# Thirty-two more bytes ahead of the weight tiles: where matmul operands start in SBUF

## The chip, the cores and the metric

The kernel runs on one core of one Trainium2 chip. The metric is the device time of one execution in microseconds (us). Three runs of the kernel before are shown, and their median is taken.

## What is computed

Two transformer blocks run one after the other on 256 tokens of width 1024, all in float32. Cut to its large products:

```
# block 1
u    = rms_norm(x, g_norm_mix);  proj = u @ w_in + b_in              # 1024 x 5408
y_m  = mlstm_mixer(...proj...);  y_n = nsa_mixer(...proj...)
x    = x + sum(sigmoid(merge) * (ys @ w_branch)) @ w_out
f    = rms_norm(x, g_norm_ffn)
x    = rms_norm(x + (silu(f @ w_gate) * (f @ w_up)) @ w_down, g_final)
# block 2
h    = rms_norm(x, g_mix_2);     z = h @ w_in_2                      # 1024 x 9304
o_gla, o_dsa, o_mem = gated linear attention, sparse attention, attention over mem
x    = x + sum(sigmoid(gate_i) * (o_i @ w_o_i)) @ w_out_2
x    = x + moe(rms_norm(x, g_ffn_2))                                 # 16 experts, 2 of one group of 4
```

## The kernel before

**Slabs.** Every large weight matrix is read in slabs of 1024 x 256 values (1 MB; 8 KB a partition). A slab lands in `ring` (four slots, `RAW`). ScalarE makes its high part `w_hi` by a copy to the rounded format fp32r (three slots, `HI`; line 580, `high`), and VectorE the low part `w_lo = ring - w_hi` over `ring` itself (line 588, `low`). The operand on the other side is kept as two such parts as well (`xT_hi`, `xT_lo`, and in other stages `ysT`, `mixT`, `memT`, `h`, `o_m`, `o_g`, `o_d`, `merged`, `xgs`, `xgo`, `turned`). TensorE adds three products for every pair, high by high, high by low, low by high (`product`, line 612, so that nearly all matmuls have this one line):

```
for m, (a, b) in enumerate(((ah, bh), (ah, bl), (al, bh))):
    ins = pe.matmul(dst, a, b, ...)      # a is loaded as 128 x 128 weights, b moves through
```

**Three ways round.** `slab_rows` loads a piece of the slab as weights and moves 256 columns of `xT` (or `ysT`, `o_m`, `o_g`, `o_d`) through it. `slab_tokens` loads a piece of the activations and moves 256 columns of the slab. `slab_wide` (stages `vo`, `memk`, `memkv`, `mq`, `gvg`, `dq`), the down projections of the FFN and the experts load activations and move 512 columns of the slab. In a profile's row the moving operand stands first: `bank<-xT_hi,w_hi` moves `xT_hi` over weights from `w_hi`.

**Stages.** `STREAM` fixes the order of the slabs: `qk`, `nq`, `kv`, `vo`, `merge`, `branch`, `out`, `memk`, then the FFN (33 slabs), `memkv` to `dq`, gates and output products of block 2, `out2`, and the experts (60 slabs). Each engine has its own program in this order. SyncE issues the loads (lines 1050 and 1117), each when a counter of slabs that TensorE is done with (`slab_used`) says that a slot is free. In the expert stage more slots are added (`ring_more`, `w_lo_more`, `w_hi_more`).

**Where tiles lie.** `sb(name, shape)` takes the next free bytes of each partition, rounded up to 32. All tiles up to `ss` have sizes that are multiples of 64 bytes. `ss` holds eight sums of squares (with the means and roots made of them) and takes 32 bytes. Behind it come `ring` (over which `w_lo` lies), `w_hi`, and the region that both blocks share, in which `place(offset, ...)` puts tiles at given distances from its start. So in the program as built (byte in the partition, and the remainder by 64 and by 256):

| tile | before | by 64 | by 256 | with the change | by 64 | by 256 |
|---|---|---|---|---|---|---|
| `x` | 22,784 | 0 | 0 | 22,784 | 0 | 0 |
| `xT_hi` | 39,168 | 0 | 0 | 39,168 | 0 | 0 |
| `xT_lo` | 47,360 | 0 | 0 | 47,360 | 0 | 0 |
| `ss` | 55,552 | 0 | 0 | 55,552 | 0 | 0 |
| `ring`, `w_lo` | 55,584 | 32 | 32 | 55,616 | 0 | 64 |
| `w_hi` | 88,352 | 32 | 32 | 88,384 | 0 | 64 |
| the region's start | 112,928 | 32 | 32 | 112,960 | 0 | 64 |
| `ysT_hi` | 209,312 | 32 | 160 | 209,344 | 0 | 192 |
| `mixT_lo` | 166,272 | 0 | 128 | 166,304 | 32 | 160 |

`memT`, `h`, `turned`, `xgs`, `xgo`, `o_m`, `o_g`, `o_d`, `merged`, `mixT_hi` and `ysT_lo` have the same remainders as the region's start. Pieces of a slab (1024 bytes apart, 512 within one) and of the activations (512 or 1024 apart) keep the remainder of their tile. `mixT_lo`, `qk`, `sig`, `v1` and `c1`, and a score of tiles of up to 128 bytes, lie behind tiles whose size is an odd multiple of 32 and so have the other remainder than the region.

Of the kernel before, what the change touches and what calls it, by code (L numbers as in the profile page):

```python
# [14 lines left out]
P = 128  # L15
T = 256
TT = T // P
# [113 lines left out]
def program(nc, dram, out, plan):  # L131
# [3 lines left out]
    def sb(name, shape, dtype=F32, into=None):  # L135
        return (into or ctx).enter_context(nc.sbuf_tensor(name, shape, dtype))
# [32 lines left out]
    with ExitStack() as into:  # L169
        xT_raw = sb("xT_raw", [P, KT, T], into=into)  # L170
    xT_lo = sb("xT_lo", [P, KT, T], F32R)
    ss = sb("ss", [P, 4 * TT])
    raw_ctx = ExitStack()
    ring = sb("ring", [P, RAW, KT, SW], into=raw_ctx)
    raw_ctx.close()
# [2928 lines left out]
```

How the kernel before makes its waits and increments, by code:

```python
    def evicted(eng, s):  # L540
        for w in all_out(s):
            eng.wait_ge(*w)
# [1 line left out]
    def slab_out(eng, name, j=0):  # L544
        eng.wait_ge(slab_used, SLAB[name] + j + 1)
# [23 lines left out]
    def high(act, end):  # L570
        for s in range(split["hi"], end):
            act.wait_ge(*loaded(s))
            if HI <= s < MOE + HI:
                act.wait_ge(slab_used, s - HI + 1)
            elif MOE + HI <= s < MOE + MORE_HI:
                act.wait_ge(*moe_pe.done("gather", KT - 1))
            elif s >= HI:
                act.wait_ge(slab_used, s - MORE_HI + 1)
            for k in halves(s):
                act.activation(HIGHS[HI_SLOT[s]][:, k, :], RAWS[SLOT[s]][:, k, :], ACT.Copy).then_inc(w_hi_ready, 1)
        split["hi"] = max(split["hi"], end)
# [1 line left out]
    def low(vec, end):  # L583
        for s in range(split["lo"], end):
            for n, k in enumerate(halves(s)):
                vec.wait_ge(w_hi_ready, parts_of(s, n))
                vec.tensor_tensor(LOWS[SLOT[s]][:, k, :], RAWS[SLOT[s]][:, k, :], HIGHS[HI_SLOT[s]][:, k, :].bitcast(F32),
                                  ALU.subtract).then_inc(w_lo_ready, 1)
        split["lo"] = max(split["lo"], end)
# [8 lines left out]
    def slab_in(pe, s):  # L599
        pe.wait_ge(w_lo_ready, parts_of(s, 0))
        if s in BANKED and BANKED[s] >= 2:
            pe.wait_ge(bank_read[BANKED[s] % 2], 2 * (BANKED[s] // 2))
# [1 line left out]
    def second_half(pe, s):  # L605
        pe.wait_ge(w_lo_ready, parts_of(s, 1))
# [431 lines left out]
    @block.sync  # L1038
# [92 lines left out]
            if name == "kv":  # L1131
                sp.wait_ge(loads["rev"], 16)
```

## Time and profile before

| | |
|---|---|
| median of three runs | 1049.6 us (1047.53 to 1049.64) |
| the profiled execution's own time | 1050.0 us |
| its span (first to last instruction) | 1048.7 us |
| instructions in the profile | 16,418 |
| mean granted TensorE clock | 0.990 of full |
| TensorE matmul, weight load: busy | 1020.1 us, 916.4 us |
| VectorE, ScalarE, GpSimd: busy | 682.9, 587.6, 36.6 us |
| moved by DMA | 203.17 MB |

The profile is of one execution. It shows matmuls as pipelined: one is shown for some 0.28 us (256 columns) or 0.40 us (512), but the next starts much earlier, so what a matmul takes of the time is the distance between two starts, called **pitch** here. It is read from the timeline, whose rows give starts to 0.01 us: over 12 to 48 matmuls in a row that is exact to a part of a nanosecond each. The chain of waits follows the work that ended last back from the end and gives the share of each line in it.

### The profile page before, as it was taken

To read this page: it belongs to the slowest core of one execution; us is meant where nothing else is said; L and a number is where in the kernel's file an instruction comes from. 1 tells how busy PE (TensorE), PEld (TensorE's weight loads), DVE (VectorE), ACT (ScalarE), POOL (GpSimd) and SP (SyncE) were. 2 spreads that over 40 slices of the span, in tenths; PEclk is the share of its full clock that TensorE was granted. 3 is DMA by queue.
4 is the path that set the end of the run, shared out by engine and by line. 5 is a ranking of instruction groups with operands and counts; after the bars stand their busy time and mean duration, and the time that the engine had idled before them with its cause. 6 is when DMAs were issued, how large, how long until landed. Compare 5 with 4: busy or idle time off the path is not lost.

```text
span 1048.7 us, 16418 instructions
## 1 busy us (share of the span) xinstructions
PE 1020.1 (97%) x6770; PEld 916.4 (87%) x6770; DVE 682.9 (65%) x1017; ACT 587.6 (56%) x859; POOL 36.6 (3%) x49
## 2 busy tenths in 40 slices
PE   6999999998999999899999999999999989999998
PEld 6988988997999999789898868999999978888886
DVE  5764767666555545566575656556555678989983
ACT  6563576645434433474585445766344557777781
POOL 4101000000000000001000001100000000000000
PEclk9999999999999999999999999999999989999999
DMA  9983543356556556555444334554555919999981
GB/s 264 269 288 93 154 156 121 124 171 183 172 190 199 175 190 201 172 168 168 147 161 126 116 121 123 176 156 147 169 182 180 321 45 315 362 357 365 366 315 41
DMA packets 167353, 203.17 MB, mean 194 GB/s; under 512 B 11304, under 2 KB 142991, under 8 KB 167279
## 3 DMA queue, kind: packets, MB, share of 16 engines
q1 hardware_dynamic: 159598, 196.01, 57.7%
q10 hardware_dynamic: 6352, 3.19, 1.2%
q0 software_dynamic: 1328, 2.92, 1.1%
q8 instruction: 54, 0.88, 0.4%
q14 instruction: 21, 0.16, 0.1%
HBM read 200.51 MB, written 2.63 MB: 194 GB/s over the span
## 4 chain that ended last, share of the span: by engine, by line
PE 92%; DVE 3%; DMA 2%; ACT 2%; issue 1%; ACTq 0%; POOL 0%; SPq 0%; DVEq 0%; POOLq 0%
PE bank L612 78%; PE bank L804 1%; PE bank L794 1%; DMA ring<-in_w_in 1%; PE bank L748 1%; PE bank L2987 1%; PE bank L3054 1%; ACT w_hi L580 1%; DVE w_lo L588 1%; PE bank L2585 1%; PE bank L2669 1%; DMA ring<-in_w_out 1%; PE bank L2724 1%; PE bank L2686 1%; DMA x<-in_x 1%
## 5 line engine op out<-in xcount | busy, mean ns | idle before, releaser
L588 DVE TENSOR_TENSOR w_lo<-ring,w_hi 128x1024 fp32r<-128x1024 f32 (+1 forms) x302 | 423.0, 1436 | 184.1 <-ACT w_hi L580 183.2
L580 ACT ACTIVATE w_hi<-ring 128x1024 fp32r<-128x1024 f32 (+1 forms) x302 | 357.4, 1225 | 185.6 <-PE bank L612 159.1
L612 PE MATMUL bank<-xT_hi,w_hi 128*128 128x256 f32 x896 | 254.3, 284 | 0.0
L612 PE MATMUL bank<-xT_hi,w_lo 128*128 128x256 f32 x896 | 251.7, 281 | 0.0
L612 PE MATMUL bank<-xT_lo,w_hi 128*128 128x256 f32 x896 | 251.6, 281 | 0.0
L612 PEld LDWEIGHTS bank<-xT_hi,w_hi 128*128 128x128 f32 x896 | 168.8, 188 | 2.5 <-issue 1.6
L612 PEld LDWEIGHTS bank<-xT_lo,w_hi 128*128 128x128 f32 x896 | 168.9, 189 | 0.8 <-issue 0.2
L612 PEld LDWEIGHTS bank<-xT_hi,w_lo 128*128 128x128 f32 x896 | 168.8, 188 | 0.0
L612 PE MATMUL bank<-w_hi,xT_hi 128*128 128x512 f32 (+1 forms) x208 | 78.8, 379 | 2.4 <-DVE v_sw L1869 2.3
L612 PE MATMUL bank<-w_hi,xT_lo 128*128 128x512 f32 (+1 forms) x208 | 77.2, 371 | 0.0
L612 PE MATMUL bank<-w_lo,xT_hi 128*128 128x512 f32 (+1 forms) x208 | 77.2, 371 | 0.0
L612 PE MATMUL bank<-w_hi,xgs_hi 128*128 128x512 f32 x128 | 52.0, 407 | 0.0
L612 PE MATMUL bank<-w_hi,xgs_lo 128*128 128x512 f32 x128 | 50.7, 396 | 0.0
L612 PE MATMUL bank<-w_lo,xgs_hi 128*128 128x512 f32 x128 | 50.6, 395 | 0.0
L612 PEld LDWEIGHTS bank<-w_hi,xT_hi 128*128 128x128 f32 x208 | 39.5, 190 | 11.5 <-DVE v_sw L1869 2.7
L612 PEld LDWEIGHTS bank<-w_hi,xT_lo 128*128 128x128 f32 x208 | 39.3, 189 | 7.4
L612 PEld LDWEIGHTS bank<-w_lo,xT_hi 128*128 128x128 f32 x208 | 39.5, 190 | 6.7
L612 PE MATMUL bank<-w_hi,h_hi 128*128 128x512 f32 x88 | 34.4, 391 | 1.4 <-issue 1.4
L612 PE MATMUL bank<-w_hi,h_lo 128*128 128x512 f32 x88 | 34.5, 392 | 0.0
L612 PE MATMUL bank<-w_lo,h_hi 128*128 128x512 f32 x88 | 34.4, 391 | 0.0
L612 PE MATMUL bank<-w_hi,memT_hi 128*128 128x512 f32 x64 | 26.0, 407 | 5.5 <-DVE w_lo L588 4.1
L612 PE MATMUL bank<-w_hi,turned_lo 128*128 128x512 f32 x80 | 31.1, 389 | 0.0
(540 smaller groups left out, 1833.4 us busy)
## 6 DMA issues: line engine op xcount, KB each, us to landing
ring<-in_w_in SPq DMA_DIRECT2D x54, 1024.0 KB, 5.3
ring<-in_w_down SPq DMA_DIRECT2D x31, 1024.0 KB, 6.6
ring<-in_w_gate SPq DMA_DIRECT2D x40, 512.0 KB, 5.5
ring<-in_w_up SPq DMA_DIRECT2D x40, 512.0 KB, 6.8
ring<-in_w_gate SPq DMA_DIRECT2D x11, 1024.0 KB, 5.4
ring<-in_w_up SPq DMA_DIRECT2D x11, 1024.0 KB, 5.4
ring<-in_w_out SPq DMA_DIRECT2D x8, 1024.0 KB, 5.4
ring<-in_w_mem_kv SPq DMA_DIRECT2D x8, 1024.0 KB, 5.1
```

The costliest lines, as they stand in the source:

```text
L580: act.activation(HIGHS[HI_SLOT[s]][:, k, :], RAWS[SLOT[s]][:, k, :], ACT.Copy).then_inc(w_hi_ready, 1)
L588: vec.tensor_tensor(LOWS[SLOT[s]][:, k, :], RAWS[SLOT[s]][:, k, :], HIGHS[HI_SLOT[s]][:, k, :].bitcast(F32), ALU.subtract).then_inc(w_lo_r ...
L612: ins = pe.matmul(dst, a, b, start=(start and j + m == 0), stop=(stop and j == len(pairs) - 1 and m == 2), **kw)
L748: ins = pe.transpose(bank[4 + k // 2][:, at:at + P], src[:, t, k * P:(k + 1) * P], ident[:, :])
L794: ins = pe.matmul(dst, a, b, start=(i == 0), stop=(i == len(parts) - 1))
L804: ins = pe.matmul(dst, a, b, start=(i == 0), stop=(i == len(parts) - 1))
L2585: ins = mm_(bank[3][0:NG * NCMP, j * P:(j + 1) * P], blk[:, j, n, :, :].rearrange("p g c -> p (g c)"), w_cmp1[:, j, n, :], start=(n == 0), ...
L2669: ins = mm_(bank[4 + odd][:, i * K:(i + 1) * K], nqT[odd * ND:(odd + 1) * ND, h // 2, tt * P:(tt + 1) * P], kT[odd * ND:(odd + 1) * ND, br ...
L2686: ins = mm_(dst[odd], v_sw[:, kt, b, g * ND:(g + 1) * ND], aT[:, b, kt, 2 * odd:2 * odd + 2, :], start=False, stop=(b == 1 and kt == tt))
L2724: ins = pe.transpose(nsa_turned(u, kt)[:, i * P:(i + 1) * P], lg_nsa(u)[:, i, kt * P:(kt + 1) * P], ident[:, :])
L2987: ins = mm_(bank[GATHER_BANK[k]][:, :], v[:, t, k * P:(k + 1) * P], onehot[:, t, 0:NGRP, :].rearrange("p g s -> p (g s)"), start=(t == 0 a ...
L3054: ins = mm_(dst, onehotT[:, g, t * P:(t + 1) * P], v[:, 4 * c:4 * c + 4, :], start=(g == 0 and n == 0), stop=(g == NGRP and n == 1), skip_ ...
```

## The change

`ss` is declared with 16 values a partition in place of 8. The added eight are never read or written. Everything behind `ss` moves up by 32 bytes, as in the table above; no instruction is added, removed, moved or changed in size on any engine.

```
     xT_lo = sb("xT_lo", [P, KT, T], F32R)
-    ss = sb("ss", [P, 4 * TT])
+    ss = sb("ss", [P, 8 * TT])
     raw_ctx = ExitStack()
     ring = sb("ring", [P, RAW, KT, SW], into=raw_ctx)
     raw_ctx.close()
     w_lo = sb("w_lo", [P, RAW, KT, SW], F32R)
     w_hi = sb("w_hi", [P, HI, KT, SW], F32R)
```

## Rows read from the trace of the kernel before

**Rows 1.** The page: busy time of each engine, share of the span, instructions.
```profile
PE 1020.1 (97%) x6770; PEld 916.4 (87%) x6770; DVE 682.9 (65%) x1017; ACT 587.6 (56%) x859; POOL 36.6 (3%) x49
```

**Rows 2.** The page: the chain that ended last, by engine and by line.
```profile
PE 92%; DVE 3%; DMA 2%; ACT 2%; issue 1%; ACTq 0%; POOL 0%; SPq 0%; DVEq 0%; POOLq 0%
PE bank L612 78%; PE bank L804 1%; PE bank L794 1%; DMA ring<-in_w_in 1%; PE bank L748 1%; PE bank L2987 1%; PE bank L3054 1%; ACT w_hi L580 1%; DVE w_lo L588 1%; PE bank L2585 1%; PE bank L2669 1%; DMA ring<-in_w_out 1%; PE bank L2724 1%; PE bank L2686 1%; DMA x<-in_x 1%
```

**Rows 3.** Groups by line and shape, line 612: count, busy us, mean ns, idle before.
```profile
L612 PE MATMUL bank<-xT_hi,w_hi 128*128 128x256 f32 x896 | 254.3, 284 | 0.0
...
L612 PE MATMUL bank<-w_hi,xT_hi 128*128 128x512 f32 x160 | 65.1, 407 | 2.3 <-DVE v_sw L1869 2.3
...
L612 PE MATMUL bank<-w_hi,xgs_hi 128*128 128x512 f32 x128 | 52.0, 407 | 0.0
...
L612 PE MATMUL bank<-w_hi,memT_hi 128*128 128x512 f32 x64 | 26.0, 407 | 5.5 <-DVE w_lo L588 4.1 <-DVE x L2105 1.4
...
L612 PE MATMUL bank<-ysT_hi,w_hi 128*128 128x256 f32 x64 | 18.5, 289 | 0.0
...
L612 PE MATMUL bank<-w_hi,xT_hi 128*128 128x256 f32 x48 | 13.7, 286 | 0.1
...
L612 PE MATMUL bank<-w_hi,xgo_hi 128*128 128x512 f32 x32 | 12.8, 400 | 0.0
```

**Rows 4.** Timeline of PE in the FFN (start us, us): first and 49th of 49.
```profile
257.50 0.28 PE L612 MATMUL bank<-xT_hi,w_hi 128*128 128x256 f32 x1
...
263.18 0.28 PE L612 MATMUL bank<-xT_hi,w_hi 128*128 128x256 f32 x1
```

**Rows 5.** Timeline of PE in `out2`: first and 49th of 49.
```profile
811.85 0.28 PE L612 MATMUL bank<-w_hi,merged_hi 128*128 128x256 f32 x1
...
817.61 0.28 PE L612 MATMUL bank<-w_hi,merged_hi 128*128 128x256 f32 x1
```

**Rows 6.** Timeline of PE in `dq`, 512 columns: first and 13th of 13.
```profile
651.10 0.40 PE L612 MATMUL bank<-w_hi,xT_hi 128*128 128x512 f32 x1
...
653.90 0.40 PE L612 MATMUL bank<-w_hi,xT_hi 128*128 128x512 f32 x1
```

**Rows 7.** Timeline of PE in `memkv`, 512 columns: first and 13th of 13.
```profile
470.09 0.39 PE L612 MATMUL bank<-w_hi,memT_hi 128*128 128x512 f32 x1
...
472.81 0.39 PE L612 MATMUL bank<-w_hi,memT_hi 128*128 128x512 f32 x1
```

**Rows 8.** Timeline of PE, `xT` as weights, 256 columns: first and 46th of 46.
```profile
614.67 0.28 PE L612 MATMUL bank<-w_hi,xT_lo 128*128 128x256 f32 x1
...
619.91 0.28 PE L612 MATMUL bank<-w_hi,xT_lo 128*128 128x256 f32 x1
```

**Rows 9.** Timeline of PE in `branch`: first and 25th of 25.
```profile
195.31 0.28 PE L612 MATMUL bank<-ysT_hi,w_hi 128*128 128x256 f32 x1
...
198.19 0.28 PE L612 MATMUL bank<-ysT_hi,w_hi 128*128 128x256 f32 x1
```

**Rows 10.** Timeline of PE in `out`: first and 25th of 25.
```profile
219.27 0.28 PE L612 MATMUL bank<-w_hi,mixT_hi 128*128 128x256 f32 x1
...
222.13 0.28 PE L612 MATMUL bank<-w_hi,mixT_hi 128*128 128x256 f32 x1
```

**Rows 11.** Groups by line and shape, VectorE.
```profile
L588 DVE TENSOR_TENSOR w_lo<-ring,w_hi 128x1024 fp32r<-128x1024 f32 x242 | 286.3, 1225 | 169.4 <-ACT w_hi L580 169.3
...
L860 DVE TENSOR_TENSOR xn<-xn,ssm 128x1024 f32<-128x1024 f32 x4 | 4.9, 1225 | 0.1
```

**Rows 12.** Groups by line and shape, ScalarE.
```profile
L580 ACT ACTIVATE w_hi<-ring 128x1024 fp32r<-128x1024 f32 x242 | 242.5, 1053 | 167.3 <-PE bank L612 151.9 <-DMA ring<-in_w_in 10.4 <-DMA ring<-in_w_out 2.8
...
L709 ACT ACTIVATE xn<-x 128x1024 f32<-128x1024 f32 x4 | 4.2, 1053 | 0.7 <-DVE x L2105 0.5 <-DVE x L2113 0.2
```

**Rows 13.** The page: DMA issues, count, KB each, median us to landing.
```profile
ring<-in_w_out SPq DMA_DIRECT2D x8, 1024.0 KB, 5.4
...
x<-in_x SPq DMA_DIRECT2D x1, 1024.0 KB, 5.4
```

More of the change, by code:

```diff
@@ L171, in program @@
     xT_lo = sb("xT_lo", [P, KT, T], F32R)
-    ss = sb("ss", [P, 4 * TT])
+    ss = sb("ss", [P, 8 * TT])
     raw_ctx = ExitStack()
```

## The prediction

> **What bounds the kernel.** I read the page from the top. TensorE is busy for 1020.1 us of a span of 1048.7, VectorE and ScalarE for 65% and 56% [rows 1]. The chain of waits agrees: 92% of it is TensorE, and 78% is the one line of the split products [rows 2]. So the time is the number of matmuls times their pitch, plus small waits. The change adds and removes no instruction. It can act only through what one instruction takes, and of the engines only TensorE's is worth much: 5640 of its 6770 matmuls are the split products on line 612.
>
> They are, by shape and by which tiles they read (every row of the groups stands for three, for the three partial products) [rows 3]:
>
> - **A**: `xT` moves, weights from the slab, 256 columns: 3 x 896 = 2688.
> - **B**: the slab moves, weights from `xT`, 256 columns: 3 x 48 = 144.
> - **C**: the same, 512 columns: 3 x 160 = 480.
> - **D**: slab and activations both from behind `ss`, 256 columns: `ysT` and five more tiles like it (`mixT`, `o_m`, `o_g`, `o_d`, `merged`), 6 x 3 x 64 = 1152.
> - **E**: the same, 512 columns: 3 x (128 + 88 + 80 + 64 + 32) = 1176, for `xgs`, `h`, `turned`, `memT`, `xgo` (three of the five groups stand there).
>
> The busy means in these rows don't tell what a matmul costs, as their ends are modelled. The timeline does, in stretches where TensorE waits for nothing:
>
> - A: 48 steps from 257.50 to 263.18, 5.68/48 = **118.3 ns** [rows 4].
> - B: 45 steps from 614.67 to 619.91, **116.4 ns** [rows 8].
> - C: 12 steps in 2.80 us, **233.3 ns** [rows 6].
> - D, with `merged`: 48 steps in 5.76 us, **120.0 ns** [rows 5].
> - E, with `memT`: 12 steps in 2.72 us, **226.7 ns** [rows 7].
>
> Here is what matters for the change. C and E are the same instruction with the same moving tile; only the tile that the weights come from differs, and the pitch differs by 6.6 ns. A and D differ by 1.7 ns. In A, B and C one operand starts at a multiple of 64 and the other at 32 past one; in D and E both start at 32 past one. So the pitch already depends on where operands lie **relative to each other**, and after the change A, B and C have both operands at multiples of 64.
>
> Two stretches say which remainder counts. `ysT_hi` lies 128 bytes further round than the slab by 256, but level with it by 64: 24 steps in 2.88 us, again 120.0 [rows 9]. `mixT_lo` is the one tile behind `ss` that is 32 off the slab by 64, and it is in a third of its stretch's matmuls: 24 steps in 2.86 us, 119.2 [rows 10], between 120.0 and A's 118.3. So the remainder by 64 seems to decide and not that by 256: level operands give 120.0 and 226.7, operands out of step 116.4 to 118.3 and 233.3. With 256 columns it is better to be out of step, with 512 columns worse.
>
> **The change, part by part.** It puts all of A, B and C level and leaves D and E level (both sides move together).
>
> - A: 2688 x (120.0 - 118.3) = 2688 x 1.7 = +4.6 us. The first nine slabs, 432 of these matmuls, run in the first 70 us, where the chain has loads of the slab and of `x` in it [rows 2]; a slab that waits for its load hides a longer pitch before it. I count half of these, 216 x 1.7 = 0.4 us, as hidden, so +4.2 us. If none hide it is +4.6.
> - B: 144 x (120.0 - 116.4) = +0.5 us.
> - C: 480 x (226.7 - 233.3) = -3.2 us.
> - D and E: 0, if a level pair at 0 costs what a level pair at 32 costs. The trace has no split product with both operands at multiples of 64, so this is the unknown. From below I bound it by the lowest pitch seen at each width (116.4 and 226.7), from above by the highest (120.0 and 233.3). I take 120.0 and 226.7, the rows of level pairs, as nearest. `mixT_lo` stays out of step.
> - VectorE: the split of a slab reads and writes tiles at 32 and takes 1225 ns for 1024 values; the softmax scaling of `xn`, at a multiple of 64, takes 1225 [rows 11]. ScalarE: 1053 for `w_hi` from `ring`, 1053 for the squares of `x` [rows 12]. Priced at zero, without any cover. The `ss` instructions keep their addresses. Some small tiles go from a multiple of 64 to 32 past one; by the same rows that costs nothing.
> - Loads: 1 MB into `ring`, at 32, lands in 5.4 us, and 1 MB into `x`, at 0, in 5.4 us [rows 13]. Zero as well, and most loads are hidden under TensorE's work; the exceptions are the few in the chain [rows 2].
>
> Sum: 4.2 + 0.5 - 3.2 = +1.5 us. The profiled execution took 1050.0 us beside a median of 1049.6, so its durations need no scaling: 1049.6 + 1.5 = 1051.1, rounded to **1051.0 us**. About 0.2% (2.1 us) is what a measurement of this kernel can tell from no change, and the forecast lies inside it.
>
> **The rivals.**
>
> 1. *An operand at a multiple of 64 has its price whatever its partner.* Then C is slow because `xT` is aligned, and not because it is out of step with the slab; after the change every 512-column product has an aligned operand and takes 233.3, and every 256-column one 118.3 (A and B stay). E: 1176 x 6.6 = +7.8 us; D: 1152 x (118.3 - 120.0) = -2.0 us. That is +5.8, **1055.4 us**, slower by 0.55%. It happens in the FFN's down products and in the experts, the last 180 us, where TensorE works without a gap. It decides if the pitch of E goes above about 228.5: 1176 x 1.8 is the 2.1 us of the threshold. For it: nothing in the trace rules it out, since no pair is at 0 and 0. Against it: the effect is the same with the aligned operand moving (A) or as weights (B), which a relation explains more simply.
>
> 2. *Both operands at multiples of 64 is the best case*, for example because a run of columns then touches one 64-byte piece less. Then every 256-column product goes to the lowest pitch seen, 116.4, and the 512-column ones to 226.7: A 2688 x -1.9 = -5.1, B 0, C -3.2, D 1152 x -3.6 = -4.1, together -12.4, **1037.2 us**. For it: A and B, with one side aligned, are both below D. Against it: C is above E, so alignment by itself has not helped at 512 columns, and 120.0 and 226.7 differ by exactly the time of 256 columns at the full 2.4 GHz, which looks like a fixed cost a matmul and no stall.
>
> 3. *The change does nothing for the pitch*: what sets A apart is a distance (by 256, from 32 now to 64 then) that stays unlike zero, or is a property of `xT` for another reason. Then A, B and C keep theirs, **1049.6 us**. For it: between the two rows of the stretch with `ysT_hi` the timeline's single steps are uneven (0.11 to 0.13 us), where those of `merged` are all 0.12 [rows 5, 9], so the remainder by 256 has some effect too. Against it: the mean over 24 steps is 120.0 all the same.
> The Trainium skill (SBUF — State Buffer, Specifications and Who interferes with whom) has 16-byte cachelines and two independent read ports for TensorE, one for the moving operand and one for weights, and says that TensorE never waits for anyone. By that rule 32 and 64 bytes are alike and the change is worth nothing, the 1049.6 us of this rival. The trace does not agree with the independence: the same moving tile takes 233.3 ns with one source of weights and 226.7 with another.
>
> **How the numbers follow.** The forecast has a chance of 0.55, rival 1 0.16, rival 2 0.14, rival 3 0.15. Rival 3 is a case of no change. The forecast's +1.5 lies 0.6 us below the threshold, and with half of A's extra either hidden or not, and medians of a few runs that range over 2 us, I give 0.41 of its 0.55 to within 0.2%, 0.13 to slower and 0.01 to faster. That makes faster 0.15, within 0.2% 0.56, slower 0.29. The range leaves out rival 2 (0.14) and takes in rival 1 with a margin of 1.6 us, hence 1057; at its lower end it has rival 3 less the bound of A and B at zero with C gained (-3.2), which is 1046.4, rounded to 1046.
>
> **What would show each step.** The timeline of the changed kernel in the FFN: 48 steps of A in 5.76 us and not 5.68 (right), in 5.6 or less (rival 2), or unchanged (rivals 1 and 3). Twelve steps of C in `dq` in 2.72 us and not 2.80; if they stay at 2.80, it is rival 1 or 3. Twelve steps of E with `memT` or `xgs` in 2.72, unchanged; 2.80 is rival 1. The stretch with `merged` stays at 5.76 for 48; 5.59 is rival 2. The means of the VectorE split (1225) and of the ScalarE copy (1053) stay; if either moves by 10 ns, or the landing of a slab by 0.3 us, I have priced the wrong engine. The prediction is wrong if level pairs at 0 don't take the pitch of level pairs at 32, or if a new wait appears in the chain.

## The result, and the profile after

The change makes the kernel faster: 1043.86 us, the median of 5 runs (1042.68 to 1044.64), beside 1049.6 us for the kernel before (5 runs, 1047.53 to 1049.86). The ratio is 0.995, with a 95% interval of 0.9935 to 0.9964. I had forecast 1051.0 us in a range of 1046 to 1057, so both the sign and the range were wrong. The profiled execution took 1044.22 us; its span is 5.8 us shorter than that of before, which is also the difference of the medians, so the two traces can be compared as they are.

The page of the kernel after, its busy times and its chain (the row of engines and the row of lines):

```profile
span 1042.9 us, 16418 instructions
...
PE 1013.5 (97%) x6770; PEld 912.3 (87%) x6770; DVE 683.4 (66%) x1017; ACT 587.7 (56%) x859; POOL 36.3 (3%) x49
...
PE 92%; DVE 3%; DMA 2%; ACT 2%; issue 1%; ACTq 0%; POOL 0%; SPq 0%; DVEq 0%; POOLq 0%
PE bank L612 78%; PE bank L804 1%; PE bank L794 1%; DMA ring<-in_w_in 1%; PE bank L748 1%; PE bank L2987 1%; PE bank L3054 1%; ACT w_hi L580 1%; DVE w_lo L588 1%; PE bank L2585 1%; PE bank L2669 1%; DMA ring<-in_w_out 1%; PE bank L2724 1%; PE bank L2686 1%; DMA x<-in_x 1%
```

The same instructions run and the chain has the same shares as before [rows 1, 2]. TensorE's busy time is 6.6 us shorter. The groups of the kernel after, by line and shape (count, busy us, mean ns), answer to rows 3, 11 and 12:

```profile
L612 PE MATMUL bank<-xT_hi,w_hi 128*128 128x256 f32 x896 | 253.1, 282 | 0.0
...
L612 PE MATMUL bank<-w_hi,xT_hi 128*128 128x512 f32 x160 | 64.9, 406 | 2.7 <-DVE v_sw L1869 2.7
...
L612 PE MATMUL bank<-w_hi,xgs_hi 128*128 128x512 f32 x128 | 52.2, 408 | 0.0
...
L588 DVE TENSOR_TENSOR w_lo<-ring,w_hi 128x1024 fp32r<-128x1024 f32 x242 | 286.3, 1226 | 166.0 <-ACT w_hi L580 165.8
...
L580 ACT ACTIVATE w_hi<-ring 128x1024 fp32r<-128x1024 f32 x242 | 242.6, 1054 | 165.8 <-PE bank L612 144.3 <-DMA ring<-in_w_in 10.5 <-issue 4.9
...
ring<-in_w_out SPq DMA_DIRECT2D x8, 1024.0 KB, 5.4
```

VectorE and ScalarE take 1226 and 1054 ns where they took 1225 and 1053, and a slab still lands in 5.4 us. As in the prediction, the modelled means of a matmul (282 for 284, 406 for 407) don't tell what it costs. The timeline does. Each pair below is the first and the last row of a stretch of the kernel after in which TensorE waits for nothing. Class A in the FFN, 48 steps:

```profile
279.82 0.28 PE L612 MATMUL bank<-xT_hi,w_hi 128*128 128x256 f32 x1
...
285.47 0.28 PE L612 MATMUL bank<-xT_hi,w_hi 128*128 128x256 f32 x1
```

Class A between 55 and 60 us, also 48 steps:

```profile
54.97 0.28 PE L612 MATMUL bank<-xT_hi,w_hi 128*128 128x256 f32 x1
...
60.41 0.28 PE L612 MATMUL bank<-xT_hi,w_hi 128*128 128x256 f32 x1
```

Class C at 634 us, 12 steps; class E with `memT`, 12 steps; class D with `merged`, 48 steps:

```profile
634.11 0.39 PE L612 MATMUL bank<-w_hi,xT_lo 128*128 128x512 f32 x1
...
636.86 0.39 PE L612 MATMUL bank<-w_hi,xT_lo 128*128 128x512 f32 x1
...
440.76 0.39 PE L612 MATMUL bank<-w_hi,memT_lo 128*128 128x512 f32 x1
...
443.48 0.39 PE L612 MATMUL bank<-w_hi,memT_lo 128*128 128x512 f32 x1
...
814.43 0.28 PE L612 MATMUL bank<-w_hi,merged_lo 128*128 128x256 f32 x1
...
820.19 0.28 PE L612 MATMUL bank<-w_hi,merged_lo 128*128 128x256 f32 x1
```

- A went from 118.3 [rows 4] to 5.65/48 = **117.7 ns** in one stretch and 5.44/48 = **113.3** in the other. It now has two steady paces. Over the 60 slabs and parts of slabs (a slab has 48 of these matmuls), 37 run at 117.8 and 23 at 113.3 to 114, and the mean is 116.3.
- C went from 233.3 [rows 6] to 2.75/12 = **229.2**.
- E with `memT` is at 2.72/12 = 226.7 [rows 7] and D with `merged` at 5.76/48 = 120.0 [rows 5], both unchanged. The mean over all products with `h` does fall, from 228.7 to 226.9, though their distance stays. Before, the first nine steps behind a slab of A take 2.08 us (231 ns each) until the pitch settles at 226.7; after, they take 2.04 us from the start:

```profile
274.54 0.40 PE L612 MATMUL bank<-w_hi,h_hi 128*128 128x512 f32 x1
...
276.62 0.39 PE L612 MATMUL bank<-w_hi,h_hi 128*128 128x512 f32 x1
```

```profile
274.03 0.39 PE L612 MATMUL bank<-w_hi,h_hi 128*128 128x512 f32 x1
...
276.07 0.39 PE L612 MATMUL bank<-w_hi,h_hi 128*128 128x512 f32 x1
```

So what runs ahead of a product counts a little as well.

Summed from start to start over the whole kernel (before, after, in us): A 321.8, 317.3; C 118.6, 117.2; `h` 63.5, 63.0; `mixT` 23.6, 23.4; B 17.1, 17.0; `memT` 45.6, 46.6. That is -4.5 - 1.4 - 0.5 - 0.2 - 0.1 + 1.1 = -5.6 us, nearly all of the 5.8. These sums hold the waits between two products too. By the pitch alone A would give 2688 x -2.0 = -5.4 us and C 480 x -4.1 = -2.0. A's missing 0.9 lies in its 384 products of the first 70 us, among the waits for loads: they took 46.4 us before and 46.3 after (45.6 and 46.7 in two more profiles of the change).

The 1.1 lost in `memT` is no pitch. It lies in a stretch in which the clock was granted at 1.2 and not 2.4 GHz. TensorE had waited for VectorE ahead of it (`xT_lo` on line 762, then `w_lo` on line 588), 4.07 us before and 4.07 us after, so the wait isn't the difference; but the low clock then lasted twice as long. From 240 to 250 us the granted clock was 0.66, where the kernel before had 0.83, and all three profiles of the change have 0.66. Why is open (window rows of the kernel before, then of the kernel after: window, length, busy us of PE, PEld, DVE, ACT, POOL with counts, granted clock, DMA share, GB/s):

```profile
240.00:250.00 10.00, 5.93 (x23) 4.63 (x20) 9.78 (x14) 4.97 (x10) 0.00 (x0) 0.83 0.75 193
```

```profile
240.00:250.00 10.00, 6.89 (x18) 5.52 (x19) 8.73 (x11) 3.46 (x6) 0.00 (x0) 0.66 0.64 163
```

### The profile page after: what moved, and what is told of

Its sections match the earlier page's. It is cut to its first block, busy times and chain, and to the rows that moved or that the text cites. A ratio compares the mean times of both kernels' runs of the same rounds, so it can differ in the third digit from the quotient of the medians.

```text
span 1042.9 us, 16418 instructions
## 1 busy us (share of the span) xinstructions
PE 1013.5 (97%) x6770; PEld 912.3 (87%) x6770; DVE 683.4 (66%) x1017; ACT 587.7 (56%) x859; POOL 36.3 (3%) x49
## 4 chain that ended last, share of the span: by engine, by line
PE 92%; DVE 3%; DMA 2%; ACT 2%; issue 1%; ACTq 0%; POOL 0%; SPq 0%; DVEq 0%; POOLq 0%
PE bank L612 78%; PE bank L804 1%; PE bank L794 1%; DMA ring<-in_w_in 1%; PE bank L748 1%; PE bank L2987 1%; PE bank L3054 1%; ACT w_hi L580 1%; DVE w_lo L588 1%; PE bank L2585 1%; PE bank L2669 1%; DMA ring<-in_w_out 1%; PE bank L2724 1%; PE bank L2686 1%; DMA x<-in_x 1%
## 5 line engine op out<-in xcount | busy, mean ns | idle before, releaser
L580 ACT ACTIVATE w_hi<-ring 128x1024 fp32r<-128x1024 f32 (+1 forms) x302 | 357.4, 1225 | 177.5 <-PE bank L612 153.5
```

The lines of the kernel that those rows point to most:

```text
L580: act.activation(HIGHS[HI_SLOT[s]][:, k, :], RAWS[SLOT[s]][:, k, :], ACT.Copy).then_inc(w_hi_ready, 1)
```

## The experiments

From here on, **distance** means the start of the weights' tile minus the start of the moving tile, by 256. Before, it is 32 in A, and -32, which is 224, in B and C; it is 0 for nearly all of D and E (`ysT_hi` is at 128 and `mixT_lo` at 96). The change makes it 64 in A and 192 in B and C. No kernel leaves out any of the work. Theory 1 is, throughout, that this distance sets the pitch; what it is set against is said with each run.

**Is it the multiple of 64, or the distance?** The kernel `moved32` has the same distances between `xT`, slabs and region as the change, but all three start at 32 past a multiple of 64 (`x` and `xn` stay at one, and `mixT_lo` comes to one):

```
-    xT_hi = sb("xT_hi", [P, KT, T], F32R)
+    sb("apart", [P, 8])
+    xT_hi = sb("xT_hi", [P, KT, T], F32R)
...
-    ss = sb("ss", [P, 4 * TT])
+    ss = sb("ss", [P, 8 * TT])
```

> The change, with all tiles from xT_hi on a further 32 bytes up: xT at 32 past a multiple of 64, slabs and region too (96 past a multiple of 256), so that no large operand starts at a multiple of 64 and the distance between xT and the slabs is 64 as with the change. Theory 1 (the distance between the moving operand and the weights decides, whatever they are multiples of): A at 113.3 or 117.8 ns a matmul, C at 229.0, time as with the change, 1043.9 us. Theory 2 (both operands at multiples of 64 is what gains): A back to 118.3, C to 233.3 or, if level by 64 counts, 120.0 and 226.7; time 1049.6 to 1051 us.

`d256` and `d128` only give `ss` 32 * TT and 16 * TT floats, so that the distance by 256 is 0 and 128, both level by 64:

> ss takes 256 bytes, so xT and slabs lie a whole 256 apart, both at multiples of 64. Theory 1, with the distance taken by 256: A and B at the 120.0 ns of merged, C at the 226.7 of memT; against the kernel before A +4.6, B +0.5, C -3.2, so 1051.5 us, and 7.6 us more than with the change. Theory 2 (multiples of 64 gain): A at 113 to 118, time near 1043.9 us.

> ss takes 128 bytes: distance 128 between xT and slabs, multiples of 64 as with the change. Theory 1: A, B, C take a third set of values, since the distance is another one; from ysT_hi at distance 128 (mean 120.0) I would say A near 120 or below, time 1044 to 1051 us. Theory 2: the same as with the change, 1043.9 us, A in its two states 113.3 and 117.8.

Measured, beside the kernel before at 1048.05 (13 runs on that chip): `moved32` 1042.94, ratio 0.9948 (0.993 to 0.9967), with A at 117.8 and 113.3 again. `d256` 1047.42, ratio 0.999 (0.9979 to 1.0001). `d128` 1048.61 in one run. The change itself, once more, 1043.38:

> The changed kernel as it is, once more. In its first profile A runs in one of two steady paces, 113.3 or 117.8 ns, by slab. If the pace is set by what stands ahead of a slab in the program (a wait of fixed length), each slab has the same pace again, and the time is 1042.7 to 1044.7 us; if it is set by chance, the slabs at 113.3 are other ones, and the time moves by up to 4.5 ns x 2688 = 12 us.

Of the 56 slabs of A, 55 have the same pace in all three profiles of the change (`after`, `after_again` and `after3` below), and the time lies in the expected range. So in this program the paces are not drawn anew each time.

The timeline of `moved32` (its line 612 is 613): class A in the FFN and between 55 and 60 us, 48 steps each.

```profile
279.94 0.28 PE L613 MATMUL bank<-xT_lo,w_hi 128*128 128x256 f32 x1
...
285.60 0.28 PE L613 MATMUL bank<-xT_lo,w_hi 128*128 128x256 f32 x1
...
54.95 0.28 PE L613 MATMUL bank<-xT_hi,w_hi 128*128 128x256 f32 x1
...
60.39 0.28 PE L613 MATMUL bank<-xT_hi,w_hi 128*128 128x256 f32 x1
```

The timeline of `d256`: class A in the FFN, 48 steps, and class C, 12 steps.

```profile
279.89 0.28 PE L612 MATMUL bank<-xT_lo,w_hi 128*128 128x256 f32 x1
...
285.65 0.28 PE L612 MATMUL bank<-xT_lo,w_hi 128*128 128x256 f32 x1
...
636.11 0.39 PE L612 MATMUL bank<-w_hi,xT_lo 128*128 128x512 f32 x1
...
638.83 0.39 PE L612 MATMUL bank<-w_hi,xT_lo 128*128 128x512 f32 x1
```

`moved32` has 5.66/48 = 117.9 and 5.44/48 = 113.3, as the change. Multiples of 64, on which the prediction built, have no part in it. `d256` has 5.76/48 = 120.0 and 2.72/12 = 226.7: exactly the values that the prediction gave to "level by 64". They belong to the distance 0, and 64 is not 0.

Its time was expected 1.9 us above the kernel before (1051.5) and came out 0.6 us below it. In its profile A does cost 5.1 us more than before (326.9 beside 321.8). But near 70 us TensorE waits 0.5 us for VectorE (`v_sw`, line 1869), where the kernel before waits 2.3, and the clock does not fall behind it: from 76 to 82 us it is granted at 1.00, where the kernel before has 0.72. That stretch differs between profiles of one and the same program too. Its rows in `after` and in `after3`, both the change:

```profile
76.00:82.00 6.00, 4.94 (x15) 3.91 (x16) 3.89 (x5) 5.02 (x12) 3.01 (x3) 0.72 0.24 74
```

```profile
76.00:82.00 6.00, 4.81 (x21) 3.98 (x22) 4.25 (x6) 5.99 (x13) 3.00 (x2) 1.00 0.37 91
```

Between matmul 450 and matmul 600 `after3` is 2.0 us shorter than `after`. So 2 us of a single time say nothing of the layout; the pitches do.

**The other distances**, by `ss` of 12, 20, 24 and 28 * TT floats:

> ss takes 96 bytes: distance 96 between xT and slabs, slabs at 32 past a multiple of 64. Theory 1 (distance): values of its own for A, B and C; if it is the size of the distance that frees the 256-column products, as good as or better than at 64 (A 113 to 118). Theory 2 (multiples of 64): as before the change, A 118.3, C 233.3, 1049.6 us.

> Distance 160, which is 96 the other way round by 256. Theory 1: near the values of distance 96 if the effect is symmetric, else its own. Theory 2: as before the change, A 118.3, C 233.3, 1049.6 us.

> Distance 192, which is 64 the other way round by 256, slabs at multiples of 64. Theory 1: values of its own, those of the change if the effect is symmetric. Theory 2: the change's values, A at 113.3 or 117.8, C 229.0, 1043.9 us.

> Distance 224, 32 the other way round by 256, slabs at 32 past a multiple of 64. Theory 1: values of its own, those of the kernel before if the effect is symmetric (A 118.3, C 233.3, 1049.6 us). Theory 2: as before, 1049.6 us.

One run each: 1048.86, 1054.1, 1046.3 and 1045.12, beside 1046.16 for the kernel before on that chip. Single runs range over 2 us or more, so it is the pitches that count here. Mean pitch in ns of the three classes in all eight kernels, each class put at its own distance (for B and C minus that of A):

```
distance            0      32     64     96     128    160    192    224
A, 256 columns    119.9  118.3  116.3  118.4  119.3  120.0  117.7  117.0
B, 256 columns    119.9  118.3  114.9  117.8  118.7  119.8  116.3  117.1
C, 512 columns    227.5  233.2  233.4  234.1  232.4  233.3  229.3  233.3
```

A and B, with the roles of `xT` and slab exchanged, fall on one curve to within some 0.6 ns except at 64 and 192, where each mean is a mixture of the same two paces, 113.3 and 117.8. Two paces are not special to these: by slab, A has 117.3 and 118.7 at 96, 118.7 and 120.0 at 128, 116.7 and 117.8 at 224, and a single pace at 0, 32 and 160. In `d128` A takes 5.70/48 = 118.8 in one stretch and 5.76/48 = 120.0 in the FFN:

```profile
43.36 0.28 PE L612 MATMUL bank<-xT_lo,w_hi 128*128 128x256 f32 x1
...
49.06 0.28 PE L612 MATMUL bank<-xT_lo,w_hi 128*128 128x256 f32 x1
...
251.08 0.28 PE L612 MATMUL bank<-xT_hi,w_hi 128*128 128x256 f32 x1
...
256.84 0.28 PE L612 MATMUL bank<-xT_hi,w_hi 128*128 128x256 f32 x1
```

With 512 columns the curve is another one: 0 is best, then 192, and the rest lies at 232 to 234. Tiles are laid out in steps of 32 bytes here, so finer distances weren't tried. That the distance counts by 256 rests on the distance 256 giving the values of 0.

**Does it hold for other tiles?** If it is the distance, then moving the region of both blocks against the slab must change D and E, which the change left alone. `region32` is the kernel before with

```
     w_hi = sb("w_hi", [P, HI, KT, SW], F32R)
+    sb("apart", [P, 8])
```

and `region192` is the change with `[P, 48]` there. `eight192` is the change with only the eight-KB places of the second block moved by 192 bytes:

```
-    EIGHT = [8 * KB + 8448 + 4608 + 8 * KB * i for i in range(11)]
+    EIGHT = [8 * KB + 8448 + 4608 + 192 + 8 * KB * i for i in range(11)]
```

> ss as before (32 bytes), and 32 bytes put between w_hi and the region: ring, w_lo and w_hi stay where the kernel before has them, only the region's tiles move, so that xT-to-slab distance is 32 as before, and the slab's distance to every region tile is 32 and no longer 0. Theory 1 (distance): A, B, C unchanged (118.3, 117, 233.3); D (o_m, o_g, o_d, ysT, merged, mixT) goes from 120.0 to near the 117.0 that xT had at distance 224, 1152 x -2.5 = -2.9 us; E (memT, h, turned, xgs, xgo) from 226.7 to near 233, 1176 x 6.3 = +7.4 us; together slower by 4.5 us, though part of the matmuls of the experts use slots in the region, which stay level: +2.5 to +4.5. Theory 2 (multiples of 64): half of the operands of D and E come to multiples of 64, nothing gained before both are there: no change.

> The change, and 192 bytes put between w_hi and the region: xT-to-slab distance 64 as with the change, and the region's tiles at multiples of 256, 64 below the slab by 256, as xT is. Theory 1: D takes the paces of A in the change, 113.3 or 117.8 in place of 120.0, 1152 x (-2.0 to -6.5) = -2.3 to -7.5 us; E takes C's 229.0 in place of 226.7, +2.7 us less what of the experts' slabs lies in region slots; against the change +0.4 to -4.8 us. Theory 2 (multiples of 64): everything is at multiples of 64 as in the change, no difference.

> The change, with only the large tiles of block 2 (the list EIGHT: o_m, o_g, o_d, merged, xgs, xgo, extra slots) 192 bytes up; memT, h, turned, ysT and mixT stay level with the slabs. Theory 1: the 768 products with o_m, o_g, o_d, merged go from 120 to 113.3 or 117.8, -1.5 to -4.9 us; the 480 with xgs and xgo from 227 to 229 where the slab is in one of the first slots, up to +1.1 us; against the change -0.4 to -4.9 us, 1039 to 1043.5. Theory 2: no difference.

> The changed kernel on the same chip as the three others, to compare them with it: 0.995 of the kernel before, by every theory.

Measured, beside the kernel before at 1048.05 (13 runs) on that chip:

| kernel | us | ratio to before (95%) |
| --- | --- | --- |
| `region32` | 1051.46 | 1.0028 (1.0017 to 1.004) |
| `after3`, the change | 1042.65 | 0.9952 (0.9935 to 0.9968) |
| `eight192` | 1040.01 | 0.9927 (0.991 to 0.9944) |
| `region192` | 1036.37 | 0.989 (0.9861 to 0.9918) |

`region32` is 3.4 us slower than before and `eight192` 2.6 us faster than the change, both inside what theory 1 expected. `region192` is 6.3 us faster than the change, where at most 4.8 was expected.

The timeline of `region192`: `o_d` (distance 64, where it was 0), 40 steps, and `h` (now 192), 12 steps.

```profile
782.62 0.28 PE L613 MATMUL bank<-o_d_hi,w_hi 128*128 128x256 f32 x1
...
787.16 0.28 PE L613 MATMUL bank<-o_d_lo,w_hi 128*128 128x256 f32 x1
...
353.20 0.39 PE L613 MATMUL bank<-w_hi,h_hi 128*128 128x512 f32 x1
...
355.94 0.39 PE L613 MATMUL bank<-w_hi,h_hi 128*128 128x512 f32 x1
```

`o_d` takes 4.54/40 = 113.5 ns and not the 119.6 of the change, `h` 2.74/12 = 228.3 (its mean over all gates is 229.7) and not 226.8. In `region32`, `h` and `memT` (distance 32) went to 233.4 and 233.3, as C has at 32; `merged` (32) to 118.2, A's 118.3; the `o` tiles (224) to 116.8, A's 117.0. So each of these tiles took, to 0.5 ns, the value that the table has for its distance. In the experts the pitches of `region32` and `region192` range from 227 to 234: there some slabs lie behind `ss` and some in the region itself, and the distance differs from slab to slab.

**Does the direction count, and is the pitch all of `region192`'s gain?** `region64` is the change with `[P, 16]` behind `w_hi`; `region192_b` repeats `region192`.

> The change, with 64 bytes more between the slab tiles and the region of both blocks (in region192 it is 192), so the weights of a product with `h` or `memT` start 64 bytes past the slab that moves over them, where they started 64 before it in region192. Theory 1, with a sign (what counts is the start of the weights minus the start of the moving tile, by 256; one curve for all tiles of a width): `h` and `memT` go to the 233.4 ns that 512 columns showed at +64 with the distance of 192 between `xT` and slab, not to the 229.3 of region192; `o_m`, `o_g`, `o_d` (weights minus moving now -64, that is 192) go to about 117.7, with 113.3 in single stretches; `merged` (+64) to 113.3 or 117.8. Against the change: -1.2 for the `o` tiles, -0.8 `merged`, -0.9 `ysT` and `mixT`, +2.9 `h` and `memT`, +1.8 the experts, about +1.8 us. Theory 2, no sign (only how far apart they are): the paces of region192, `h` and `memT` 229.3, `o_d` 113.3, and region192's time.

> region192 once more, beside region64 and in more rounds. The single pitches of region192, summed against the change on that chip, gave -2.0 us, its median -6.3. Theory 1 (the pitches are the whole): the runs lie about 2 to 3 us below the change, 1040 to 1041. Theory 2 (the shorter stretches of a lower granted clock that its profile showed, 0.89 to 0.94 from 230 to 250 us where the change had 0.66, belong to it): again 1036 to 1037, and again the higher clock in that stretch.

Measured, beside the kernel before at 1047.56 (9 runs): `region64` 1043.09, ratio 0.9944 (0.9924 to 0.9963); `region192_b` **1032.56**, ratio **0.986** (0.9834 to 0.9886), 5 runs of 1031.32 to 1038.24. The timeline of `region64`: `h` (distance 64), 12 steps; `merged` (64), 48 steps; `o_d` (192), 40 steps.

```profile
356.96 0.39 PE L613 MATMUL bank<-w_lo,h_hi 128*128 128x512 f32 x1
...
359.76 0.39 PE L613 MATMUL bank<-w_lo,h_hi 128*128 128x512 f32 x1
...
804.51 0.28 PE L613 MATMUL bank<-w_hi,merged_hi 128*128 128x256 f32 x1
...
809.95 0.28 PE L613 MATMUL bank<-w_hi,merged_hi 128*128 128x256 f32 x1
...
776.89 0.28 PE L613 MATMUL bank<-o_d_hi,w_lo 128*128 128x256 f32 x1
...
781.60 0.28 PE L613 MATMUL bank<-o_d_hi,w_hi 128*128 128x256 f32 x1
```

`h` takes 233.3, `merged` 113.3 and `o_d` 117.8, all three as theory 1 said. The direction counts: weights 64 bytes past the moving tile and weights 64 bytes ahead of it are two different cases. The time came out near the change (0.9952 of the kernel before, on another chip) and not 1.8 us above it. In the profile that is because eleven more slabs of A ran at 113.3 to 114 (34 of 60), though the distance of A was the same as in the change.

The pace of a slab repeats from one profile of the change to the next, but it isn't fixed by the program: the two profiles of `region192` differ in it for 30 of the 56 slabs. The windows of `region192`, first profile:

```profile
240.00:440.00 200.00, 197.26 (x1369) 183.32 (x1367) 109.35 (x125) 79.80 (x100) 0.70 (x1) 0.99 0.57 182
740.00:820.00 80.00, 80.00 (x709) 80.00 (x707) 51.31 (x66) 40.46 (x57) 0.00 (x0) 1.00 0.73 237
```

and of the second profile, `region192_b`:

```profile
240.00:440.00 200.00, 197.26 (x1389) 182.65 (x1389) 114.25 (x133) 84.73 (x106) 0.70 (x1) 1.00 0.58 189
740.00:820.00 80.00, 80.00 (x683) 80.00 (x683) 49.08 (x64) 39.31 (x56) 0.00 (x0) 1.00 0.70 233
```

In the FFN the second has 20 matmuls more in the same 200 us (all 22 slabs of A there at 113.3, those of the first all at 117.8); between 740 and 820 us it has 26 fewer (117.8 in `o_d`, `merged` and the slabs of A between them, the first 113.3). The start of the same matmul in the two profiles, counted from TensorE's first, minus the same in the profile `after3` of the change, in us, worked out from the timelines:

```
matmul no.                   525    1750   1800   3000   4650   5850   5990   6750
region192                   -3.0   -3.1   -4.0   -3.3   -3.0   -7.0   -9.2   -7.5
region192_b                 -2.4   -2.5   -3.6   -7.2   -7.2   -8.0   -8.2   -6.4
```

So theory 1 of `region192_b`, the pitches counted once, was too small, and the median, 1032.56, lies below theory 2's 1036 to 1037 as well. In the two profiles the gain has these parts:

- 2.4 to 3.0 us lie before matmul 525, in the first 79 us. Of these, 1.6 to 1.9 are waits: `after3` waits 2.9 us there (for `v_sw`, and for `cmp_in` on ScalarE), the two profiles 1.0 and 1.3. That the layout shortens this wait is not shown; `d256`, where D and E lie at 0 as in the change, waits 0.5.
- Some 4 us come in whichever part runs at 113.3: the output products of the second block in the first profile, the FFN in the second.
- About 1 us at matmul 1800 and, in the first profile, 2.1 between 5850 and 5990 lie where the clock stood at 1.2 GHz for less long.
- `h` and `memT`, at 229 and not 227, give back up to 1 us, and the experts 1.7 to 1.9.

The higher clock at 230 to 250 us was there again in the second profile (0.90 from 240 to 250, after 0.89), as theory 2 had it, but it is one part of several. Its row of the first profile, and then that of `after3`:

```profile
240.00:250.00 10.00, 10.00 (x58) 8.87 (x57) 6.57 (x6) 4.42 (x6) 0.00 (x0) 0.89 0.37 115
```

```profile
240.00:250.00 10.00, 8.41 (x27) 6.73 (x28) 7.21 (x8) 2.65 (x4) 0.00 (x0) 0.66 0.45 100
```

The profiled executions took 1035.04 and 1035.99 us. Those of 1031 to 1033 us have no profile, so what made them faster still is not known.

## Why the prediction was wrong

- **The step that failed** is the reading of the two uneven stretches: "So the remainder by 64 seems to decide and not that by 256: level operands give 120.0 and 226.7". Neither stretch can carry it. That of `ysT`, 120.0 [rows 9], has `ysT_hi` at the distance 128 in two thirds of its products, and `d128` shows that A at 128 runs at 120.0 in some slabs and at 118.7 in others, with a mean of 119.3: the stretch has one of the two paces, and could not tell "level by 64" from "128 by 256". That of `mixT`, 119.2 [rows 10], has `mixT_lo` at the distance 96, where A takes 118.4, in a third of them: two thirds of 119.9 and a third of 118.4 are 119.4. So the remainder by 256 accounts for both. I had even noted the uneven single steps as a sign that the remainder by 256 matters, and gave that rival 0.15 with no change of the pitch, though an unlike distance may just as well have an unlike pitch. At a distance of 64 the pitch is 116.3 and 229.3 and not 120.0 and 226.7.
- **A** was to cost +4.2 us and gave -4.5. **C** was to give -3.2 and gave -1.4, or -2.0 by its pitch alone: the sign was right and the size was not. **B** was to cost +0.5 and gave -0.1. The counts of matmuls were right and the prices were those of another distance: with `d256`, which has that distance, A took 120.0 and C 226.7. Even there the sum of these prices, +1.9, did not show in the time, 1047.42, which can't be told from before. The sum takes waits and clock as unchanged, and between `after` and `after3`, the same program, they differ by 2.0 us.
- **The hidden part of A** was put at 432 products of the first 70 us, half of them hidden. There are 384, and as said above nearly all of what their pitch changed was taken up by waits. **B**'s price came from one stretch of 116.4 [rows 8]; its mean before is 117.1.
- **D and E at 0** was right: pairs level at 0 take what pairs level at 32 take, 120.0 and 226.7. Rival 1 (1055.4), an aligned operand with a price of its own, is out. So is the reason of rival 2 (both at multiples of 64), by `moved32`; its sum for A, -5.1, was near the measured -4.5 by accident, and its -4.1 for D came out at 0 with `merged` and the `o` tiles.
- **VectorE, ScalarE and loads at zero** was right: 1 ns more for either engine's split, and 5.4 us for a slab to land as before.
- The Trainium skill (SBUF — State Buffer, Who interferes with whom) gives TensorE two read ports, one for the moving operand and one for weights, that are independent. Taken as a rule for the pitch, that would leave all pitches alone. The runs are against it: with nothing but the distance changed, A goes from 113.3 to 120.0 and C from 226.7 to 234.
- The lower end of the range, 1046, was too high, because the range left out rival 2 (0.14), the one case with A gaining. Rows of before spoke for such a gain: B, at 116.4, is the same operation at another distance, and A at 116.4 with C gained would have been 2688 x -1.9 - 3.2 = -8.3 us.

## What to carry to other kernels

Where TensorE is the bound and its matmuls are paced by pairs of weight load and matmul, write down for each class the start of the weights minus the start of the moving tile, by 256, and try a few paddings; these values are of fp32r products with a weight load each. In this kernel 64 was best for 256 columns (113.3 or 117.8 ns against 120.0) and 0 for 512 (226.7 against 233), and a few bytes of padding set it. Change one distance at a time and read the pitch in the timeline, because the mean of a group doesn't show it. The whole gain is small (the change 0.5%, with `region192` 1.1 to 1.4%), and a tile that serves both widths must be weighed by its counts.

## What the hardware showed that I had not expected

- The pitch of a matmul in fp32r depends here on the distance between its two tiles, seen in steps of 32 bytes and by 256, in a curve that isn't symmetric: with 512 columns 192 gives 229.3 and 64 gives 233.4.
- With 256 columns there are two steady paces at five of the eight distances. At 64 and 192 they are 113.3 ns (256 columns at the full 2.4 GHz take 106.7, so 6.6 on top) and 117.8. A slab nearly always keeps its pace to its end, and passes it to the next where nothing comes between. It can change after a wait. In the change 55 of 56 slabs repeat their pace in all three profiles, but in `region192` the same stretch of the same program ran at 113.3 in one profile and at 117.8 in the next. That is worth some 4 us here and may be why `region192` ranges over 6 to 7 us (1031.32 to 1038.24) where the kernel before ranges over 3 to 4. What picks the pace is open. No run was made that holds all but the entry to a slab fixed, and 227 ns products ahead of the FFN's slabs aren't needed for the slow pace, since with 229 ns ahead of them the first profile of `region192` had 117.8 too.
- Why the distance counts at all is open as well. That weight load and moving reads meet in the same part of the memory would fit, but no view here shows it.
